# Making the first gates and four expert blocks of the dense half while the gathered half is still being ranked

## The reference

```python
for i in range(DEPTH):
    mod = (c_act @ ada_w[i] + ada_b[i])[:, None, :]
    sh1, sc1, g1, sh2, sc2, g2 = jnp.split(mod, ADA_CHUNKS, axis=-1)
    h = _rmsnorm(x, norm_mix_g[i]) * (1.0 + sc1) + sh1
    ...
    x = x + g1 * m
    h = _rmsnorm(x, norm_ffn_g[i]) * (1.0 + sc2) + sh2
    x = x + g2 * _peer(h, pk_w_q[i], pk_keys[i], pk_u[i], pk_v[i])
return _rmsnorm(x, final_g)

def _peer(h, w_q, sub_keys, u_tab, v_tab):
    q = (hf @ w_q).reshape(T, PEER_HEADS, 2, PEER_DQH)           # 8 heads
    s = jnp.einsum('thcd,hcnd->thcn', q, sub_keys)               # 2 x 128 keys
    top_s, top_i = lax.top_k(s, PEER_TOPK)                       # 16 of each
    cand = (top_s[:, :, 0, :, None] + top_s[:, :, 1, None, :]).reshape(...)
    best_s, best_c = lax.top_k(cand, PEER_TOPK)                  # 16 of 256
    ...
    experts = i1 * N_KEYS + i2                                   # of 16384
    gates = jax.nn.softmax(best_s, axis=-1)
    # y[t] = sum over 128 picks: gelu(u_tab[e] . h[t]) * gate * v_tab[e]
```

## Time and profile before

| what | value |
|---|---|
| median of 3 runs | 3539.59 us (3537.83 to 3540.31) |
| the profiled execution: its own time / its span | 3545.07 us / 3543.3 us |
| PE busy | 3179.2 us (90%), mean granted clock 0.921 |
| DVE busy | 2502.8 us (71%) |
| ACT busy / POOL busy | 479.0 us (14%) / 1254.0 us (35%) |
| moved by DMA | 957.18 MB, mean 270 GB/s |

### The profile page before, as it was taken

One profiled execution on the slowest core, in us unless ns is written; L12 is line 12 of the kernel. 1 busy time (PEld: TensorE's weight loads), 2 busy tenths in 40 slices (PEclk: granted clock), 3 DMA queues, 4 the chain that ended last, 5 costly groups with the idle time before them and its releaser, 6 DMA issues.

```text
span 3543.3 us, 44528 instructions
## 1 busy us (share of the span) xinstructions
PE 3179.2 (90%) x12852; PEld 2291.5 (65%) x12852; DVE 2502.8 (71%) x5303; ACT 479.0 (14%) x1062; POOL 1254.0 (35%) x1168
## 2 busy tenths in 40 slices
PE   7899869699999999999979897838999999999996
PEld 3685746596776766555568784737877676655554
DVE  0397899778888886666623586397788888766665
ACT  0211211010000000000043215201100000000001
POOL 0000000105555557777500000002255555677773
PEclk9899979659999999999979999975699999999998
DMA  8234315319999999999922340213399999999996
GB/s 313 87 133 170 114 64 180 131 32 388 410 403 409 406 406 410 410 410 410 372 84 97 118 143 12 85 59 100 114 410 407 406 401 409 405 410 410 410 410 262
DMA packets 242900, 957.18 MB, mean 270 GB/s; under 512 B 26953, under 2 KB 27129, under 8 KB 225146
## 3 DMA queue, kind: packets, MB, share of 16 engines
q0 software_dynamic: 147456, 536.94, 38.5%
q1 hardware_dynamic: 95354, 419.17, 31.2%
HBM read 953.90 MB, written 2.10 MB: 270 GB/s over the span
## 4 chain that ended last, share of the span: by engine, by line
PE 53%; DMA 16%; issue 12%; DVE 11%; ACT 4%; POOL 3%; DVEq 0%; POOLq 0%; ACTq 0%; SPq 0%
DMA v_rows<-in_pk_v,idx_now 14%; PE out_e L727 13%; PE acc L718 13%; PE acc L488 11%; PE mid L708 6%; PE acc L480 4%; DVE mod_rows L1290 2%; POOL v_rows L426 1%; DVE scratch L1309 1%; POOL u_rows L420 1%; DMA u_rows<-in_pk_u,idx_now 1%; PE mid L679 1%; PE out_e L510 1%; DMA weights<-in_ada 1%; DVE scratch L1306 1%
## 5 line engine op out<-in xcount | busy, mean ns | idle before, releaser
L727 PE MATMUL out_e<-weights,mod_rows 128*128 128x512 f32 x2048 | 932.4, 598 | 61.6 <-DVE mod_rows L1335 59.7
L718 PE MATMUL acc<-h_t,weights 128*128 128x256 f32 x4096 | 933.8, 381 | 0.0
L718 PEld LDWEIGHTS acc<-h_t,weights 128*128 128x128 f32 x4096 | 784.0, 192 | 217.8 <-issue 123.5
L426 POOL DMA_INDIRECT v_rows<-in_pk_v,idx_now x512 | 630.5, 1231 | 606.0 <-DVE mod_rows L1290 484.9
L1290 DVE SCALAR_TENSOR_TENSOR mod_rows<-v_rows,acts,mod_rows 128x1024 f32<-128x1024 f32 x512 | 657.9, 1285 | 199.0 <-DMA v_rows<-in_pk_v,idx_now 195.5
L1273 DVE SCALAR_TENSOR_TENSOR u_rows<-u_rows,h_rows 128x1024 f32<-128x1024 f32 x512 | 625.8, 1222 | 82.5 <-DMA u_rows<-in_pk_u,idx_now 81.7
L727 PEld LDWEIGHTS out_e<-weights,mod_rows 128*128 128x128 f32 x2048 | 377.2, 190 | 468.1 <-issue 368.0
L420 POOL DMA_INDIRECT u_rows<-in_pk_u,idx_now x512 | 564.6, 1103 | 292.4 <-issue 142.3
L415 POOL COPY idx_now<-pick_idx 128x8 int32 (+1 forms) x128 | 56.2, 439 | 1348.2 <-DVE pick_gate L1268 1300.5
L708 PEld LDWEIGHTS mid<-scratch 128*128 128x128 f32 x2048 | 338.6, 257 | 20.2 <-DVE scratch L1309 16.9
L708 PE MATMUL mid<-scratch 128*128 128x64 f32 x2048 | 341.4, 343 | 10.6 <-DVE scratch L1309 10.6
(11 more groups left out here) (184 smaller groups left out, 2072.0 us busy)
## 6 DMA issues: line engine op xcount, KB each, us to landing
weights<-in_u_t SPq DMA_DIRECT2D x256, 512.0 KB, 6.7
weights<-in_pk_v SPq DMA_DIRECT2D x256, 512.0 KB, 6.7
weights<-in_ada SPq DMA_DIRECT2D x42, 1024.0 KB, 4.9
weights<-in_pk SPq DMA_DIRECT2D x32, 1024.0 KB, 4.8
weights<-in_w_qkv SPq DMA_DIRECT2D x24, 1024.0 KB, 4.8
weights<-in_w_in SPq DMA_DIRECT2D x16, 1024.0 KB, 4.8
weights<-in_w_out SPq DMA_DIRECT2D x8, 1024.0 KB, 4.9
u_rows<-in_pk_u,idx_now POOLq DMA_INDIRECT x512, 10.9
```

Of the source, the lines that this page charges most:

```text
L426: nc.gpsimd.indirect_dma_start(v_rows[:, r % VR, :], None, a["pk_v"], bass.IndirectOffsetOnAxis(ap=idx_now[:, 1, par, r:r + 1], axis=0)).t ...
L718: last = nc.tensor.matmul(acc[s][:, 0:HALF], weights[:, s, k * P:(k + 1) * P], h_t[:, k, :], start=k == 0, stop=k == KB - 1)
L727: last = nc.tensor.matmul(out_e[2 * tt + c][:, :], e_act[:, s, tt * P:(tt + 1) * P], weights[:, s, D + c * 512:D + (c + 1) * 512], start=F ...
```

## The change

1. **adaLN moved up.** In `CHAIN` and on PE the last 12 adaLN chunks come ahead of the norm and the queries of the gathered half of layer 0; ACT's copy, DVE's bias (`add_bias`) and column spread go with them. `mod_cols` gets a set for each layer.
2. **Transposes and round 0's gates moved up.** The transposes of the dense half's picks (`picks_t`) come after the third head's queries of h = 1, and the 32 groups of gates (`first_gates`, in four parts of 8) between the queries of heads 3 to 7, on PE, ACT and DVE alike (`rank_and_gates` on DVE: heads 0 and 1, then four times 8 groups and one head). They use `out_e[2]` and `out_e[3]`; the queries of h = 1 are staged in `g1_row` instead of `scratch`.
3. **Four expert blocks moved up.** Blocks 0 to 3 of round 0 are multiplied by their gates during and after the ranking of heads 6 and 7 (`midway` of `rank`). From then on the batches are shifted: batch b of the picks goes with the blocks of batch b + 1, the last batch of round 0 with the first four blocks of round 1, and the last batch of the layer with none.
4. **The dot products of the first batch** now stand alone, after the softmax of the gathered half; they were between the groups of gates.

The diff, cut to its core:

```diff
-          ("pk", 0, 0, range(8)), ("out", 0, 1, range(4)), ("pk", 0, 1, range(8)), ("ada", 1, 4, range(12, 24)),
+          ("pk", 0, 0, range(8)), ("out", 0, 1, range(4)), ("ada", 1, 4, range(12, 24)), ("pk", 0, 1, range(8)),
...
+                    sp.wait_ge(acc_full, full("pk", l, 1, 6 + s))
...
+            def picks_t(l):
+
+                pe.wait_ge(picks_ready, 4 * l + 2)
                 pe.wait_ge(mod_ready, 2)
                 for m in range(3):
+                    to = out_e[1][:, m * HALF:(m + 1) * HALF] if m < 2 else out_e[0][:, 0:HALF]
                     for tt in range(2):
                         src = pick_key[:, tt, m, :] if m < 2 else pick_gate[:, 0, tt, :]
-                        at = m * HALF + tt * P
-                        last = nc.tensor.transpose(mid[at // 512][:, at % 512:at % 512 + P], src, ident[:, :])
+                        last = nc.tensor.transpose(to[:, tt * P:(tt + 1) * P], src, ident[:, :])
                 last.then_inc(picks_t_full, 1)
+
+            def gates_group(l, i, s, to):
+                n = i * 2 + (l * ROUNDS * GROUPS + s)
+                pe.wait_ge(hots_ready, n + 1)
+                pe.wait_ge(gates_ready, n + 1)
+                for t in range(GROUP):
+                    last = nc.tensor.matmul(to[:, t * ROUND:(t + 1) * ROUND], hot2[:, s, t, :], hot1[:, s, t, :],
+                                            start=True, stop=True)
+                last.then_inc(gates_full, 1)
+
+            def first_gates(l, r):
+
+                for n in range(8 * r, 8 * r + 8):
+                    gates_group(l, n // 2, n % 2, out_e[2 + n % 2])
+
+            def peer(l):
+
+                pe.wait_ge(gates_ready, (l * ROUNDS + 1) * GROUPS + CREDIT)
...
+            ada(1, 12, 12)
             norm(0, 1, 1)
-            select(0, 1)
-            ada(1, 12, 12)
-            spread_columns(1)
+            select(0, 1, {0: lambda: spread_columns(1), 2: lambda: picks_t(0)} |
+                   {3 + r: lambda r=r: first_gates(0, r) for r in range(4)})
             peer(0)
 
...
+            def first_gates(l, r):
+                for n in range(8 * r, 8 * r + 8):
+                    act.wait_ge(gates_full, l * ROUNDS * GROUPS + n + 1)
+                    nc.scalar.activation(gates_0[:, :, n * GROUP:(n + 1) * GROUP],
+                                         out_e[2 + n % 2][:, :].rearrange("p (t i) -> p i t", t=GROUP), ACT.Copy
+                                         ).then_inc(gates_ready, 1)
...
+                blocks(0, 0)
+                exps(l, 1)
                 row_gelu(2 * l, 0)
+                with act.Fori(0, BATCHES - 1) as b:
+                    blocks(0, b + 1)
+                    row_gelu(2 * l, b + 1)
+                blocks(1, 0)
...
+            def rank_and_gates(l):
+                rank(l, 1, 0)
+                if l == 0:
+                    softmax(0, 0)
+                rank(l, 1, 1)
+                dve.wait_ge(picks_t_ready, l + 1)
+                for r in range(4):
+                    for n in range(8 * r, 8 * r + 8):
+                        hots(l, 0, n // 2, n % 2)
+                    rank(l, 1, 2 + r)
+                dve.wait_ge(gates_ready, (l * ROUNDS + 1) * GROUPS + CREDIT)
+                for n in range(2):
+                    rank(l, 1, 6 + n, lambda: weigh_block(l, 0, 0, 2 * n))
+                    steps.settle()
+                    weigh_block(l, 0, 0, 2 * n + 1)
+                less_best(1)
+                softmax(l, 1)
...
+                def batch(q, b, blocks, after):
+                    weigh(q, b)
+                    for n in range(PER_BATCH):
+                        if blocks:
+                            weigh_block(l, *blocks, n)
+                        for r in range(n * BATCH // PER_BATCH, (n + 1) * BATCH // PER_BATCH):
+                            if after:
+                                u_dot(*after, r)
+                            v_add(q, b, r)
+                    if after:
+                        dots_done(*after)
+
...
+                        batch(q, b, (g, b + 1), (q, b + 1))
+                    if g == 0:
+                        dve.wait_ge(gates_ready, (l + 1) * ROUNDS * GROUPS + CREDIT)
+                    batch(q, BATCHES - 1, (1, 0) if g == 0 else None, (q + 1, 0) if g == 0 else None)
...
+            add_bias(1)
             rank(0, 0, 7)
             less_best(0)
-            for head in range(PH):
-                rank(0, 1, head)
-            less_best(1)
-            softmax(0, 0)
-            softmax(0, 1)
             spread_columns(1)
+            rank_and_gates(0)
             peer(0)
```

More of the change, by code:

```diff
@@ L731, in peer @@
                 u_block(0, 0)
-                with pe.Fori(0, GROUPS // 2) as i:
-                    for s in range(2):
-                        gates_group(i, s)
                 with pe.Fori(0, ROUND // 4) as i:
@@ L808, in _ @@
             norm(1, 1, 1)
-            select(1, 1)
+            select(1, 1, {2: lambda: picks_t(1)} | {3 + r: lambda r=r: first_gates(1, r) for r in range(4)})
             peer(1)
@@ L1075, in _ @@
             norm(1, 1, 1)
-            select(1, 1)
-            exps(1, 1)
+            select(1, 1, {2: lambda: picks_t(1)} | {3 + r: lambda r=r: first_gates(1, r) for r in range(4)})
             peer(1)
@@ L1434, in _ @@
             gather_rows(1, 1)
-            for head in range(PH):
-                rank(1, 1, head)
-            less_best(1)
-            softmax(1, 1)
+            rank_and_gates(1)
             peer(1)
```

166 lines of the change are left out of this document (64 added, 102 removed).

## The result

| | median | lowest to highest | runs |
|---|---|---|---|
| before | 3539.95 us | 3537.83 to 3540.50 | 4 |
| changed | 3559.51 us | 3553.82 to 3561.30 | 4 |

The ratio is 1.0054, 95% interval 1.0036 to 1.0071: the change makes the kernel **slower by some 20 us**. The forecast was 3545 with a range of 3514 to 3567, and 3531 to 3560 for its own case. The time lies in both, at the upper edge of the second. The forecast's words, "no measurable change, leaning to slower", did not come true: 20 us can be measured. Of the three chances the largest, slower with 0.39, did.

What follows compares the result with a forecast made beforehand. Round 0's batches were taken as bound by PE's lockstep, round 1's by DMA. The terms 23.5 + 3 + 6 - 27 = +5.5 us gave 3550.6 from the profiled 3545.07, or a median of 3545, range 3514 to 3567.

Steps and rivals of the forecast that it cites:

- its own case: The forecast's main case for the whole kernel: +5.5 us, own range 3531 to 3560 us, chance 0.66.
- the three chances: For the whole kernel against the one before: faster 0.26, same 0.35, slower 0.39; same meant within 7 us.
- The adaLN delay: Layer 0, ahead of the gathered half's ranking: the moved adaLN chunks make that ranking start 23.5 us later.
- The stretch: From the start of the gathered half's ranking to the first batch's weigh: +3 us in layer 0, +6 in layer 1.
- behind the first batch: From the first batch to the layer's end: shorter last batches, less dense DMA, fewer prefetched rows; together -13.5 us per layer.
- -11: After the last weigh of each layer: the last batch has no dense blocks, so its tail takes 14.5 us, 11 less.
- another 3.5: In the batch before the last, which runs out of dense loads: 3.5 us less per layer.
- +1 for rows that have not landed: At the start of each layer's batches: fewer rows are prefetched, but DMA is running by then; costs 1 us.
- -27: The saving behind the first batch, -13.5 us for each layer, as it entered the sum over both layers.
- The clock holds through the gates: Rival for the moved gates: each part takes 21 us at full clock, -48 in all, about 3498 us; chance 0.10.
- The DMA stretch shrinks by more: Rival for the batches: 20 us less per layer instead of 13.5, time 3528 to 3535 us; chance 0.10.
- The rows are not there when the batches start: Rival for the first batches: DMA never makes up missing prefetched rows, 11 us lost per layer, about 3567 us; chance 0.14.

Runs made afterwards that it cites:

- again: The changed kernel once more, unaltered, timed in turns with the kernel before: 3565.7 us, ratio 1.0062 to the kernel before.
- layer 1 only: The new order in layer 1, with layer 0 in the order of the kernel before: 3538.4 us, ratio 0.9980 to that kernel.
- adaLN only: The kernel before with only the twelve adaLN chunks and ACT's copy moved ahead of the gathered half's second norm: 3565.1 us, ratio 1.0069.
- layer 0 only: The new order in layer 0, adaLN chunks moved up, with layer 1 as in the kernel before: 3567.0 us, ratio 1.0062 to that kernel.
- the run with the dense pairs: The kernel before, in its old order, with two dense 128x256 matmuls, never read, behind each group of round 0's gates: 3508.7 us, ratio 0.9891.
- the one with the spread adaLN: The changed kernel with seven adaLN chunks ahead of the norm, five among queries and gates, zero matmuls behind the first u_block: 3522.4 us, 0.9951 of the kernel before.

## Why the prediction was right and wrong

**The mechanism held.** The adaLN delay, forecast at +23.5, is 23.3 to 28.1 in the profiles of the seven runs that have it (lead of 162.0 to 166.4 for 138.3 to 138.7; 163.4 in the one with dense matmuls among the moved gates), and 24 by the time of the run that has nothing else. The spread among them is in the chunks: from the first to the end of the twelfth they took 50.8 to 54.3 us, PE waiting 7.2 to 9.3 of it for their loads. DVE's idle 22.14 was forecast as some 22.

**The stretch.** Forecast +3 and +6, measured +2.0 and +8.0 (again: +2.4 and +8.2). The four parts of gates, from the first table to the end of the eighth, take DVE 26.8, 26.1, 25.9 and 25.9 in layer 0 and 26.8 each in layer 1: 104.7 and 107.2 where I had 108. The wait ahead of the first L1327 was 5.86, not 3.7: the zero matmuls took 4.6 there, not 3.7, and the u_block behind them, which I had at full clock, ran its first 3.5 us at 0.50. From the softmax's end to the first weigh it was 21 instead of 18 to 20. These small misses nearly cancel.

**The term that was mis-sized** is "behind the first batch ... together -13.5 for each layer". It measured -8.5 in layer 0 (tail -8.1, batches -0.4) and -12.7 in layer 1 (-10.9 and -1.8); again, -6.5 and -11.4. Of it, the "-11" for the last batch was 8 to 9 in layer 0, 10 to 11 in layer 1. The "another 3.5" for the batch before the last was seen in that batch (28.3 and 25.5 us for 30.7 before). What ate it up is at the other end. The first four batches together took 121.7 and 122.1 us instead of 119.1 and 119.2 (again: 123.0 and 121.9), where I had +1 for rows that have not landed. They had landed: DVE waited for no row there, but 18.6 us in layer 0 for ACT's Gelu of the blocks, where before it was 12.0 for that and 3.6 for rows. PE's lockstep of 31.1 us a batch, which before came in after three batches of 27.4, 30.3 and 30.3, now holds from the second batch on. In place of my -27 stand -21 in the first profile and -18 in the second.

**Where the rest went.** By the measured terms the sum is +24.0 + 2.0 + 8.0 - 8.5 - 12.7 = +12.8 for the first profile and, in the same way, +24.6 + 2.4 + 8.2 - 6.5 - 11.4 = +17.3 for the second; the medians' difference is +19.6, with an interval from 13 to 25. The two profiled executions of before and changed gave only +8.8: that of before, at 3545.07, lay 5.1 over its median, and that of the changed kernel was the fastest of its four, 5.7 below its own. Some 4 of the 11 between +8.8 and +19.6 lie in places that the change does not touch (3.2 ahead of the first MAX8, 1.1 between the layers). The rows that the sum was made against are steady: where the old order stands, the stretch is 254.6 and 254.5 again in layer 0 (layer 1 only, adaLN only) and 249.4 twice in layer 1 (layer 0 only, adaLN only). That leaves up to 7 us between rows and medians which no row of one profile can place, and half of the way from +5.5 to +19.6 with it. That part stays open.

**The rivals.** "The clock holds through the gates" did not happen: 0.50 to 0.55. "The DMA stretch shrinks by more" did not: it shrank by less. "The rows are not there when the batches start" would have shown as batches 11 us longer in each layer; in the changed kernel's two executions they are between 1.8 less and 2.5 more than before, and DVE waited for no row in the first four. The side, slower, came from the forecast's own terms. That the time fell within that case's range, 0.5 us from its edge, owes something to luck: its sum was 14 us short.

**What I did not weigh.** I named the clock as a rival of the changed kernel and never as what the kernel before loses. By the run with the dense pairs, half clock costs its gates 21 us in each layer; the best order that ran without them won 19 in both together. The old order with full clock needs 233.8 and 228.6, the changed order at half clock 256.6 and 257.4. I also read the fall in the earlier trace rows as one "in the middle of gate work", with PE busy nearly all the time; the wait of 1.83 us right ahead of it I had overlooked, though the fall comes with less too (0.47). The Trainium skill ("TensorE: Matmul & The Clock Gate", Part 1) says that matmul activity releases the throttle and idle time brings it back. The traces agree only in part: PE was busy 28.00 of 28 us with gates at 0.50, and with two dense matmuls behind each group it was at 1.00 while it was busy *less*, 22.36 of 24. In the moved order, where PE idles 2.6 us or more ahead of a part, windows over the parts with the same dense work showed 0.75 to 0.93. So it is not the waits alone: gates alone lost the clock with waits of 0.36 and 0.47 us and did not get it back with waits of 0.2 us between pairs of groups, the zero matmuls lost it while PE was busy all the time, and the dense pairs kept it with waits of 0.78. The kind of matmul counts. What exactly in it (the columns, the share of weight loads, the operands) these runs do not settle.

## What to carry to other kernels

Work that has been hidden costs its full length when it is moved ahead of the operation that everyone waits for. Before you move a block to make room, look for PE's idle stretches on either side of it: seven chunks fitted into the norm's wait and five among the queries and gates; that and the zero matmuls behind the first u_block turned a loss of 20 us into a gain of 19. And read the granted clock beside the busy share: an engine that is 96% busy at half clock is worth an experiment before its work is moved. Here two lines that compute nothing gained 37 us, the best reordering 19.

## What the runs showed of the hardware

- A part of eight groups with one dense matmul in each ran either at 1.00 or near 0.50 almost from end to end, 20.8 to 22.2 or 29.0 to 30.8 us, with the same instructions; three of eight parts were at the upper level, those ahead of which PE had waited least (1.25 us at most; 2.15 or more ahead of the others).
- With two dense matmuls in each group, the old order, in which PE waited 0.8 us at most between groups, was at 1.00 in the windows of its gates; the new order, which idles ahead of each part, was not.
- Gates alone lost the clock after a wait of 1.83 us in the kernel before, and after waits of 0.36 and 0.47 us in the one with the spread adaLN; before, they then stayed at 0.50 for the rest of round 0's gates, some 108 us. With a dense pair in each group the clock held through waits of 0.78 us, and where it was down it came back in the midst of a part.
- Over four matmuls that fill PSUM with zeros from one row each (1x128 by 512 columns), PE busy all the time, the clock fell from 1.00 too (0.79 and 0.78 over them).
- Executions of the same early program differ by up to 9 us before the change's place: layer 0's first MAX8 came between 394.0 and 402.9 in the profiles, and those two are of one chip. One profile against one profile does not place a change of 0.2%.
